# VectorE's late routing work between parts of its expert loop, and two weight parts and x0's low rows moved in the prologue

## The chip, the cores and the metric

The kernel runs on one core of one Trainium2 chip. The metric is the device time of one execution in microseconds; the kernel before takes 1338.12 us as the median of 3 runs (1337.47 to 1338.19).

## What is computed

The reference is one encoder layer over 512 tokens of width 1024, in float32, and a final norm:

```
h = x + W_out [ ConformerConv(xn) ; NeighbourhoodAttn2D(xn) ] + b_out,   xn = rmsnorm(x)
xt = rmsnorm(h);  logits = xt @ w_router + b_router
top 4 of 32 experts for each token, gates = softmax of the four logits
gt = min(xb @ w_gate[e] + b_gate[e], 7);  up = clip(xb @ w_up[e] + b_up[e], -7, 7)
y  = ((up + 1) * gt * sigmoid(1.702 gt)) @ w_down[e] + b_down[e]
h  = h + sum over the four experts of gate * y;   out = rmsnorm(h)
```

Each expert has three 1024 x 1024 float32 matrices, 12 MB; all 32 experts are read once, about 403 MB.

## The kernel before

**Stages.** Up to about 215 us the kernel does the input projections, the convolution and the attention. Then PE multiplies by W_out, tile by tile (`project_attn`, `project_conv`), VectorE adds the residual and norms (`residual`, `norm2`), PE turns the tiles and computes the router's logits, and VectorE picks the four best (`top`). From these VectorE sorts the experts by their token counts (big ones at even places of the order, small ones of at most 64 tokens at odd places), works out for each token and expert its rank, its block and its place in the block, and PE turns one-hot matrices into a token table (`table`). The expert part follows.

**Pieces.** An expert's weights are 12 pieces of 1 MB: 4 of gate, 4 of up, 4 of down. SyncE loads a piece into `w_raw` (`load`, line 486); ScalarE casts it to fp32r, `w_high` (`high_part`, line 833, a ring of 4 places, so it is at most 3 pieces ahead of PE); VectorE subtracts, `w_low` = `w_raw` - `w_high`, in place (`low_part`, line 1283). PE then takes three products for a piece of a big expert, high x high, low x high, high x low (`piece`, lines 1936 to 1938), and two for a piece of a small one (`piece_small`, lines 1952 and 1953). There are 12 buffers of raw pieces; SyncE reloads a buffer when PE counts its piece as used (`piece_used`).

**The order of the expert part.** Each engine has its instructions in an order written out by hand, and the engines meet at semaphores. Gate and up of expert 0 come first (a peeled stretch), then a pass for each expert j: gate and up of j+1, then down of j. Even and odd passes differ (`dve_even`, `dve_odd` on VectorE, `act_even`, `act_odd` on ScalarE), and a loop of 14 turns takes a pair each; the last passes are peeled again. GpSimd gathers the next expert's tokens with an indirect DMA, PE transposes them, ScalarE and VectorE split them into high and low rows (`xT_low_part`, for expert 0 `x0T_low`).

**What the change touches.** In the prologue: ScalarE's `high_part(1, 0, 1)` stands after the third tile's work and `high_part(2, 0, 2)` after the last tile's; VectorE's `low_part(1, 1)` stands between `xn2T_first(3)` and `top(2)`; `low_part(2, 2)` and `xT_low_part(0)` stand after the rank chain (`packed_i`, `parts_i`, `pos`), ahead of the one-hot matrices. ScalarE loads b_down over the bias staging area (line 842) before the first `square2`, and g_final (line 893) after the softmax of the gates. In the peeled stretch of expert 0 VectorE runs, beside its low parts: `dense_gates` (i = 0), `list_overflow` (i = 1, lines 1444 to 1451), `order_experts` (i = 2, lines 1565 to 1577), `split_down_bias` (i = 3, line 1455). In pass 0 it runs `late_onehots` (lines 1607 to 1610). Only the end of the kernel reads what these make (the addition of the experts' rows, the overflow blocks, the bias of down), but for `dense_gates`. SyncE waits for `list_overflow` before it loads piece 10 of expert 0.

Of the kernel before, what the change touches and what calls it, by code (L numbers as in the profile page):

```python
# [5 lines left out]
F32 = mybir.dt.float32  # L6
# [8 lines left out]
P = 128  # L15
SEQ, D_MODEL = 512, 1024
# [44 lines left out]
def encoder_kernel(nc, x, g_mix, w_in, b_in, conv_w, conv_b, ln_g, ln_b, rpb, w_out, b_out,  # L61
# [3 lines left out]
    with ctx:  # L65
# [90 lines left out]
        def split_parts(g):  # L156

            if g >= 16:
# [36 lines left out]
        gffn_row = area_v[:, 0:1024]  # L195
        gfin_row = area_a[:, 0:1024]
        xg = area_m[:, 0:1024]
        row_order = [(0, n) for n in range(NQ)] + [(r, n) for n in range(NQ) for r in range(1, TOP_K)]
# [31 lines left out]
                                   for i, name in enumerate(("first_slot", "pos_i", "slot")))  # L230
        ovf_exp = over("ovf_exp", t_at, 2048 + 3 * NJ, [1, MAX_OVERFLOW], I32)

        slot_of_rank = over("slot_of_rank", t_at, 2128, [P, NJ], I32)
# [3 lines left out]
        rank_j = area_t[:, 2128 + 4 * NJ + 64:2128 + 5 * NJ + 64]  # L237
        place_j, rank, first_j, extra_j, is_extra, blk, pos, tmp_j = (area_q[:, NJ * i:NJ * (i + 1)] for i in range(8))
        key, key_junk, place_off = (area_k[:, 32 * i:32 * i + 32] for i in range(3))
# [5 lines left out]
        parts_i = over("parts_i", k_at, 336, [P, 3, NJ], I32)  # L245
        counts, n_extra, first_extra, ovf_exp_f = (area_q[:, 128 + 32 * i:160 + 32 * i] for i in range(4))
        ovf_exp_f = ovf_exp_f[0:1, 0:MAX_OVERFLOW]
        cum = area_q[:, 256:256 + 4 * N_EXPERTS].rearrange("p (b e) -> p b e", b=2)

# [84 lines left out]
        wout_low_ready = sem("wout_low_ready")  # L334
        wout_done = sem("wout_done")
        wout_high_ready = sem("wout_high_ready")
        conv_high_ready = sem("conv_high_ready")
# [119 lines left out]
        def _(sp):  # L457
# [54 lines left out]
            for i in range(GATE, DOWN):  # L512
                if i == UP:
                    sp.wait_ge(overflow_ready, 2)
                    sp.wait_ge(gate_rows_ready, 1)
                    load(10, 0)
                reload(i, second, i)
# [174 lines left out]
        def _(act):  # L692
# [146 lines left out]
            s.copy(bias_gu[64:128, :], bias_stage[64:128, :]).then_inc(bias_high, 1)  # L839
            act.wait_ge(bias_split, 2)  # L840
            for i in range(4):
                act.dma_start(bias_stage[32 * i:32 * i + 32, :], b_down[0]).then_inc(bias_rows_loaded, 16)

            def square2(n):
# [9 lines left out]
            def xn2T_half(n):  # L854
                act.wait_ge(xn2_transposed, 2 * n + 2)
                s.copy(xn2T[n // 2][:, n % 2, 4:8, :],
                       bank[2 * (n % 2) + 1][:, :].rearrange("p (k t) -> p k t", k=4)).then_inc(xn2T_act, 1)

            square2(0)
            square2(1)  # L860
# [8 lines left out]
            act.wait_ge(wout_done, 2 * NQ)  # L869
            high_part(1, 0, 1)  # L870
            xn2_out(3)
# [11 lines left out]

            high_part(2, 0, 2)
            act.wait_ge(logits_done, NQ)
# [6 lines left out]
            act.wait_ge(xn2_stored, 16 * NQ)  # L892
            act.dma_start(gfin_row, row_bcast(g_final, D_MODEL)).then_inc(norm_rows_loaded, 16)
            act.wait_ge(bias_rows_loaded, 128)
            s.copy(bias_d[:, :], bias_stage).then_inc(bias_high, 1)

# [121 lines left out]
            with act.Fori(0, N_EXPERTS // 2 - 2) as jj:  # L1018
                act_odd(2 * jj + 1)
                act_even(2 * jj + 2, jj + 1)  # L1020
            act_odd(N_EXPERTS - 3, turn_small=False)
            act_even(N_EXPERTS - 2, N_EXPERTS // 2 - 1, last=True)
# [32 lines left out]
        def _(dve):  # L1055
# [225 lines left out]
            def low_part(i, at, raw=0):  # L1281
# [9 lines left out]
                            ALU.subtract).then_inc(bias_split, 1)  # L1291

            dve.wait_ge(norm_rows_loaded, 16)
            dve.wait_ge(router_loaded, 32)
# [18 lines left out]
            xn2T_first(3)  # L1313
            low_part(1, 1)
            top(2)
# [83 lines left out]
            then(v.tensor_reduce(packed_f, picked, AX.X, ALU.add))  # L1399
            then(v.tensor_copy(packed_i[:, :], packed_f))  # L1400
            v.tensor_scalar(parts_i[:, 1, :], packed_i[:, :], 1023, None, ALU.bitwise_and)
            v.tensor_scalar(parts_i[:, 2, :], packed_i[:, :], 15, None, ALU.logical_shift_right)
            then(v.tensor_scalar(upper_i[:, :], packed_i[:, :], 10, None, ALU.logical_shift_right))
            then(v.tensor_scalar(parts_i[:, 0, :], upper_i[:, :], N_EXPERTS - 1, None, ALU.bitwise_and))
            then(v.tensor_copy(area_q[:, 0:3 * NJ], parts_i[:, :, :].rearrange("p a b -> p (a b)")))

# [3 lines left out]
            then(v.scalar_tensor_tensor(pos[:, :], extra_j[:, :], -float(CAP), rank[:, :], ALU.mult, ALU.add))  # L1410
            low_part(2, 2)
            dve.wait_ge(xg_transposed, 1)
            xT_low_part(0, x0T_high, x0T_low)
            v.tensor_tensor(pos_1h[:, :, :], across(iota_f[:, 0:CAP], NJ), wide(pos[:, :], CAP), ALU.is_equal).then_inc(onehots_ready, 1)
# [27 lines left out]
            def list_overflow():  # L1442
                dve.wait_ge(gate_rows_ready, 1)
                v.tensor_scalar(first_slot[:, :], blk[:, :], float(CAP), None, ALU.mult)
                v.tensor_copy(pos_i[:, :], pos[:, :]).then_inc(slot_ready, 1)

                v.tensor_copy(n_ovf[:, :], cum[0:1, cur, 2 * N_EXPERTS - 1:]).then_inc(overflow_ready, 1)
                seen = cmp[0:1, :].rearrange("p (b e) -> p b e", e=N_EXPERTS)
                then(v.tensor_tensor(seen, wide(iota_f[0:1, 0:MAX_OVERFLOW], N_EXPERTS), across(cum[0:1, cur, N_EXPERTS:], MAX_OVERFLOW), ALU.is_ge))
                then(v.tensor_reduce(ovf_exp_f[:, :], seen, AX.X, ALU.add))  # L1450
                v.tensor_scalar(ovf_exp[:, :], ovf_exp_f[:, :], N_EXPERTS - 1.0, None, ALU.min).then_inc(overflow_ready, 1)

            def split_down_bias():
                dve.wait_ge(bias_high, 3)
                v.tensor_tensor(bias_d[32:64, :], bias_stage[32:64, :], bias_d[32:64, :].bitcast(F32),
                                ALU.subtract).then_inc(bias_split, 1)
# [101 lines left out]

            def order_experts():
# [4 lines left out]
                ranks = iota_f[:, 0:TOP_K].unsqueeze(1).unsqueeze(3).to_broadcast([P, NQ, TOP_K, TOP_K])  # L1564
                ranked(v.scalar_tensor_tensor(slot_f, blk[:, :], float(CAP), pos[:, :], ALU.mult, ALU.add))
# [4 lines left out]
                ranked(v.tensor_tensor(flat_gates, flat_gates, tmp_j[:, :], ALU.mult))  # L1570
                ranked(v.tensor_tensor(slot_f, slot_f, tmp_j[:, :], ALU.mult))
                ranked(v.tensor_tensor(earlier, inner(rank_j), ranks, ALU.is_equal))
                ranked(v.tensor_tensor(picked_rank, earlier, inner(slot_f), ALU.mult))
# [5 lines left out]
            for i in range(DOWN):  # L1579
# [3 lines left out]
                if i == 0:  # L1583
                    dense_gates()
                if i == 1:
                    list_overflow()
                if i == 2:
                    order_experts()
                if i == 3:
                    split_down_bias()  # L1590
                if i == 5:
                    xS_low_part(1)
                if i == 4:
                    dve.wait_ge(bias_split, 3)
                    dve.wait_ge(gate_rows_turned, 1)
                    v.tensor_copy(gate_cols[:, :, :], bank[4].rearrange("p (n t) -> p n t", n=NQ)).then_inc(gate_cols_ready, 1)
# [9 lines left out]
            def late_onehots():  # L1606
                know(v.tensor_reduce(row_gate, bank[5][:, COLS:COLS + 4].rearrange("p (b s) -> p b s", b=2), AX.X, ALU.add))
                know(v.tensor_copy(row_tok, tok_tab[:, LATE:N_EXPERTS]))
                for n in range(NQ):
                    know(v.tensor_scalar(row_tile[:, :, n], row_tok, -float(n * P), None, ALU.add))  # L1610
# [18 lines left out]
            dve_even(0, 0)  # L1629
            with dve.Fori(0, N_EXPERTS // 2 - 2) as jj:  # L1630
                dve_odd(2 * jj + 1)
                dve_even(2 * jj + 2, jj + 1)
            dve_odd(N_EXPERTS - 3, turn_small=False)
# [54 lines left out]
        def _(pe):  # L1688
# [96 lines left out]
            def project_attn(n):  # L1785
# [348 lines left out]
```

## Time and profile before

| | |
|---|---|
| median of 3 runs | 1338.12 us |
| the profiled execution | 1338.11 us, span 1336.3 us |
| PE busy | 1269.6 us (95%) |
| VectorE (DVE) busy | 1227.8 us (92%) |
| ScalarE (ACT) busy | 972.3 us (73%) |
| moved by DMA | 473.31 MB, mean 354 GB/s |

Busy times are shares of the whole span, over stages with different limits; a busy PE is not PE at its peak, since the ends of matmuls are modelled. DMA share is the mean busy share of the core's 16 DMA engines. A time in brackets behind an instruction is how long its engine sat idle before it, and what ended that. All times of rows are from the span's start.

### The profile page before, as it was taken

To read this page: it belongs to the slowest core of one execution; us is meant where nothing else is said; L and a number is where in the kernel's file an instruction comes from. 1 tells how busy PE (TensorE), PEld (TensorE's weight loads), DVE (VectorE), ACT (ScalarE), POOL (GpSimd) and SP (SyncE) were. 2 spreads that over 40 slices of the span, in tenths; PEclk is the share of its full clock that TensorE was granted. 3 is DMA by queue.
4 is the path that set the end of the run, shared out by engine and by line. 5 is a ranking of instruction groups with operands and counts; after the bars stand their busy time and mean duration, and the time that the engine had idled before them with its cause. 6 is when DMAs were issued, how large, how long until landed. Compare 5 with 4: busy or idle time off the path is not lost.

```text
span 1336.3 us, 17611 instructions
## 1 busy us (share of the span) xinstructions
PE 1269.6 (95%) x5771; PEld 1011.6 (76%) x5771; DVE 1227.8 (92%) x1010; ACT 972.3 (73%) x788; POOL 182.7 (14%) x181
## 2 busy tenths in 40 slices
PE   4999889789999999999999999999999999999996
PEld 4887668667878778787777777878777777777775
DVE  6799956699999999999999999999999999999997
ACT  4241664448797978788888888797979787878762
POOL 5001000112010101010110102020101010101252
PEclk9999889889999999999999999999999999999999
DMA  9945401499999999999999999999999999999984
GB/s 284 389 170 142 157 1 52 150 365 400 397 401 422 409 421 409 419 410 421 409 420 409 417 410 422 408 418 414 409 419 411 422 409 418 407 419 421 408 319 157
DMA packets 83974, 473.31 MB, mean 354 GB/s; under 512 B 10059, under 2 KB 10358, under 8 KB 34790
## 3 DMA queue, kind: packets, MB, share of 16 engines
q1 hardware_dynamic: 71726, 436.57, 81.1%
q0 software_dynamic: 7072, 19.39, 4.6%
q10 hardware_dynamic: 5144, 16.93, 3.4%
q8 instruction: 18, 0.29, 0.1%
q14 instruction: 14, 0.11, 0.0%
HBM read 447.72 MB, written 29.33 MB: 357 GB/s over the span
## 4 chain that ended last, share of the span: by engine, by line
PE 69%; DVE 15%; DMA 6%; ACT 5%; issue 3%; ACTq 1%; SPq 0%; POOL 0%; DVEq 0%
PE pair L1936 14%; PE pair L1937 13%; PE pair L1938 13%; PE pair L1952 6%; PE pair L1953 6%; DMA w_raw<-in_w_up 6%; DVE w_low L1283 5%; DVE area_m L1134 4%; ACT w_high L833 2%; PE pair L1923 2%; PE pair L1971 2%; PE pair L1950 1%; PE pair L1714 1%; PE pair L1715 1%; PE pair L1716 1%
## 5 line engine op out<-in xcount | busy, mean ns | idle before, releaser
L1283 DVE TENSOR_TENSOR w_low<-w_raw,w_high 128x2048 fp32r<-128x2048 f32 x380 | 838.2, 2245 | 41.3 <-ACT w_high L833 40.0
L833 ACT CAST w_high<-w_raw 128x2048 fp32r<-128x2048 f32 x380 | 703.0, 1878 | 170.5 <-PE pair L1938 117.5
L1936 PE MATMUL pair<-w_high,xT_high 128*128 128x512 f32 x528 | 211.2, 400 | 0.0
L1937 PE MATMUL pair<-w_low,xT_high 128*128 128x512 f32 x528 | 206.6, 391 | 0.0
L1938 PE MATMUL pair<-w_high,xT_low 128*128 128x512 f32 x528 | 206.0, 390 | 0.0
L1952 PE MATMUL pair<-w_high,xS 128*128 128x512 f32 x450 | 183.3, 407 | 0.1
L1953 PE MATMUL pair<-w_low,xS 128*128 128x512 f32 x450 | 175.7, 390 | 0.0
L1936 PEld LDWEIGHTS pair<-w_high,xT_high 128*128 128x128 f32 x528 | 99.1, 188 | 31.9 <-issue 11.4
L1938 PEld LDWEIGHTS pair<-w_high,xT_low 128*128 128x128 f32 x528 | 99.2, 188 | 21.6
L1937 PEld LDWEIGHTS pair<-w_low,xT_high 128*128 128x128 f32 x528 | 99.2, 188 | 19.2
L1936 PE MATMUL pair<-w_high,hT_high 128*128 128x512 f32 x256 | 102.1, 399 | 11.1 <-DVE w_low L1283 11.1
L1952 PEld LDWEIGHTS pair<-w_high,xS 128*128 128x128 f32 x450 | 84.5, 188 | 21.8 <-issue 3.6
L1937 PE MATMUL pair<-w_low,hT_high 128*128 128x512 f32 x256 | 100.5, 393 | 0.0
L1938 PE MATMUL pair<-w_high,hT_low 128*128 128x512 f32 x256 | 100.3, 392 | 0.0
L1953 PEld LDWEIGHTS pair<-w_low,xS 128*128 128x128 f32 x450 | 84.6, 188 | 20.4 <-issue 3.6
L1952 PE MATMUL pair<-w_high,hS 128*128 128x512 f32 x240 | 95.0, 396 | 0.0
L1953 PE MATMUL pair<-w_low,hS 128*128 128x512 f32 x240 | 93.5, 389 | 0.0
L1134 DVE SCALAR_TENSOR_TENSOR area_m<-area_u,convT,area_m 128x512 f32<-128x512 f32 x120 | 84.0, 755 | 0.4
L615 POOL CAST sel_in<-is_expert 128x128 fp32r (+1 forms) x17 | 42.6, 2504 | 272.0 <-PE pair L1953 246.9
L1936 PEld LDWEIGHTS pair<-w_high,hT_high 128*128 128x128 f32 x256 | 48.4, 189 | 23.7 <-DVE w_low L1283 12.2
L618 POOL CAST shift_sel<-is_expert 64x64 fp32r x15 | 14.1, 938 | 362.3 <-PE pair L1938 354.1
L1938 PEld LDWEIGHTS pair<-w_high,hT_low 128*128 128x128 f32 x256 | 48.5, 189 | 10.4
(355 smaller groups left out, 1800.5 us busy)
## 6 DMA issues: line engine op xcount, KB each, us to landing
w_raw<-in_w_gate SPq DMA_DIRECT2D x128, 1024.0 KB, 15.5
w_raw<-in_w_up SPq DMA_DIRECT2D x128, 1024.0 KB, 16.9
w_raw<-in_w_down SPq DMA_DIRECT2D x128, 1024.0 KB, 16.8
ring<-in_w_in SPq DMA_DIRECT2D x5, 2048.0 KB, 18.7
y_rows<-area_t SPq DMA_DIRECT2D x1, 8704.0 KB
y_rows<-area_m ACTq DMA_DIRECT2D x15, 512.0 KB
ring<-in_w_out SPq DMA_DIRECT2D x2, 2048.0 KB, 7.9
y_rows<-area_t SPq DMA_DIRECT2D x1, 3840.0 KB, 38.6
```

The lines of the kernel that those rows point to most:

```text
L615: g.tensor_copy(sel_in[:, :], is_expert[:, bass.ds(e, 1)].to_broadcast([P, CAP])).then_inc(sel_in_ready, 1)
L618: g.tensor_copy(shift_sel[SMALL:, SMALL:], is_expert[SMALL:, bass.ds(e, 1)].to_broadcast([SMALL, SMALL])).then_inc(sel_in_ready, 1)
L833: s.copy(w_high[:, i % HIGH_RING, raw:], w_raw[i][:, raw:]).then_inc(high_ready, 1)
L1134: v.scalar_tensor_tensor(mixedT[:, c, :], u_pad[:, c, k:k + SEQ], convT[:, k * CC + c:k * CC + c + 1], mixedT[:, c, :], ALU.mult, ALU.add) ...
L1283: v.tensor_tensor(w_low[i][:, raw:], w_raw[i][:, raw:], w_high[:, i % HIGH_RING, raw:].bitcast(F32), ALU.subtract).then_inc(low_ready, 1)
L1923: last = t.transpose(bank[6 + k // 4][:, (k % 4) * CAP:(k % 4 + 1) * CAP], h_tok[:, k::KD], ident[0:CAP, 0:CAP])
L1936: t.matmul(to[half], tok_high, hi, start=(opens and kk == 0), stop=False)
L1937: t.matmul(to[half], tok_high, lo, start=False, stop=False)
L1938: last = t.matmul(to[half], tok_low, hi, start=False, stop=(k == KD - 1))
L1952: t.matmul(to[half], rows, w_high[:, i % HIGH_RING, cols], start=(opens and kk == 0), stop=False)
L1953: last = t.matmul(to[half], rows, w_low[i][:, cols], start=False, stop=(k == KD - 1))
L1971: t.matmul(to[half], sel[:, :], rows[:, half * HALF:(half + 1) * HALF], start=True, stop=False)
```

## The change

Five things are done:

- VectorE's loop of 14 pairs is cut into six loops (3, 2, 3, 2, 2 and 2 pairs). Between them stand `late_rows` (the last five instructions of the old `late_onehots`), `list_overflow`, `order_by_rank` and `slots_by_rank` (together the old `order_experts`), and `split_down_bias`. What they read and write moves from area_q to area_v and area_t, where the loop doesn't overwrite it.
- The cast and the subtraction of weight piece 1 move ahead of the first `square2` and the first residual, behind a new semaphore that PE raises when the attention half of W_out is done. Those of piece 2 take the place that piece 1's had.
- `xT_low_part(0)` moves up, ahead of the unpacking of the ranks.
- SyncE no longer waits for the overflow list before it loads piece 10.
- The load of b_down moves into the place of that of g_final, into a part of area_a (`down_stage`); that of g_final goes behind ScalarE's loop. PE waits for the bias split only before it opens the output tiles.

```
@@ SyncE
                 if i == UP:
-                    sp.wait_ge(overflow_ready, 2)
                     sp.wait_ge(gate_rows_ready, 1)
                     load(10, 0)
@@ ScalarE, before the first square2
-            act.wait_ge(bias_split, 2)
-            for i in range(4):
-                act.dma_start(bias_stage[32 * i:32 * i + 32, :], b_down[0]).then_inc(bias_rows_loaded, 16)
+            act.wait_ge(attn_projected, NQ)
+            high_part(1, 0, 1)
             square2(0)
...
             act.wait_ge(wout_done, 2 * NQ)
-            high_part(1, 0, 1)
+            high_part(2, 0, 2)
             xn2_out(3)
             xn2T_half(3)
-            high_part(2, 0, 2)
...
             act.wait_ge(xn2_stored, 16 * NQ)
-            act.dma_start(gfin_row, row_bcast(g_final, D_MODEL)).then_inc(norm_rows_loaded, 16)
+            act.wait_ge(xn2_transposed, 2 * NQ)
+            for i in range(4):
+                act.dma_start(down_stage[32 * i:32 * i + 32, :], b_down[0]).then_inc(bias_rows_loaded, 16)
             act.wait_ge(bias_rows_loaded, 128)
-            s.copy(bias_d[:, :], bias_stage).then_inc(bias_high, 1)
+            s.copy(bias_d[:, :], down_stage).then_inc(bias_high, 1)
@@ ScalarE, behind its loop
+            act.wait_ge(bias_split, 3)
+            act.dma_start(gfin_row, row_bcast(g_final, D_MODEL)).then_inc(norm_rows_loaded, 16)
             act_odd(N_EXPERTS - 3, turn_small=False)
@@ VectorE
+            low_part(1, 1)
             dve.wait_ge(norm_rows_loaded, 16)
...
             xn2T_first(3)
-            low_part(1, 1)
+            low_part(2, 2)
             top(2)
...
             then(v.tensor_copy(packed_i[:, :], packed_f))
+            dve.wait_ge(xg_transposed, 1)
+            xT_low_part(0, x0T_high, x0T_low)
             v.tensor_scalar(parts_i[:, 1, :], packed_i[:, :], 1023, None, ALU.bitwise_and)
...
-            low_part(2, 2)
-            dve.wait_ge(xg_transposed, 1)
-            xT_low_part(0, x0T_high, x0T_low)
             v.tensor_tensor(pos_1h[:, :, :], ...).then_inc(onehots_ready, 1)
...
                 if i == 0:
                     dense_gates()
-                if i == 1:
-                    list_overflow()
-                if i == 2:
-                    order_experts()
-                if i == 3:
-                    split_down_bias()
...
             dve_even(0, 0)
-            with dve.Fori(0, N_EXPERTS // 2 - 2) as jj:
-                dve_odd(2 * jj + 1)
-                dve_even(2 * jj + 2, jj + 1)
+            def dve_pairs(first, end):
+                with dve.Fori(first, end) as jj:
+                    dve_odd(2 * jj + 1)
+                    dve_even(2 * jj + 2, jj + 1)
+
+            dve_pairs(0, 3)
+            late_rows()
+            dve_pairs(3, 5)
+            list_overflow()
+            dve_pairs(5, 8)
+            order_by_rank()
+            dve_pairs(8, 10)
+            slots_by_rank()
+            dve_pairs(10, 12)
+            split_down_bias()
+            dve_pairs(12, N_EXPERTS // 2 - 2)
@@ PE, project_attn
-                        t.matmul(to, attn_low[:, k, tokens], wout_high[half][:, 4 + k, :], start=False, stop=False)
+                        last = t.matmul(to, attn_low[:, k, tokens], wout_high[half][:, 4 + k, :], start=False, stop=False)
+                last.then_inc(attn_projected, 1)
@@ PE, before the output tiles
             pe.wait_ge(late_1h_ready, 1)
+            pe.wait_ge(bias_split, 3)
```

## Rows read from the trace of the kernel before

**Rows 1.** The page: DMA busy tenths in 40 slices; DMA issues.

```profile
DMA  9945401499999999999999999999999999999984
...
area_a<-in_g_final ACTq DMA_DIRECT2D x1, 512.0 KB, 3.8
area_m<-xn_rows,tok_now POOLq DMA_INDIRECT x32, 8.8
```

**Rows 2.** Windows: length, busy times, PE clock, DMA share, GB/s.

```profile
288.00:290.00 2.00, 2.00 (x11) 1.63 (x10) 1.93 (x4) 1.26 (x1) 1.01 (x1) 1.00 0.85 197
...
350.00:1270.00 920.00, 910.51 (x4088) 725.35 (x4087) 879.00 (x463) 774.62 (x506) 117.01 (x89) 1.00 1.01 414
```

**Rows 3.** DMA issues in 363:426, 900:963, 1128:1192; last number: us to landing.

```profile
w_raw<-in_w_gate SPq DMA_DIRECT2D x8, 1024.0 KB, 9.6
...
w_raw<-in_w_gate SPq DMA_DIRECT2D x8, 1024.0 KB, 19.3
...
w_raw<-in_w_gate SPq DMA_DIRECT2D x8, 1024.0 KB, 21.2
```

**Rows 4.** The chain that ended last: start us, us, what.

```profile
384.22 1.93 ACT w_high L833
...
447.49 1.92 ACT w_high L833
...
1081.27 1.92 ACT w_high L833
...
1145.69 1.92 ACT w_high L833
...
1186.19 19.20 DMA w_raw<-in_w_up
```

**Rows 5.** Waits in 1128:1192: total us, times, longest.

```profile
ACT w_high L833 <- DMA w_raw<-in_w_gate: 1.8, 3, 1.0
```

**Rows 6.** Timeline 268 to 275: start, us, engine, line, op, tiles.

```profile
268.98 1.01 ACT L951 CAST x0T_high<-pair 128x1024 fp32r<-128x1024 f32 x1 [8.15 <-PE pair L1916]
269.03 0.18 DVE L1400 CAST packed_i<-area_k 128x16 int32<-128x16 f32 x1
...
270.73 2.29 DVE L1283 TENSOR_TENSOR w_low<-w_raw,w_high 128x2048 fp32r<-128x2048 f32 x1
272.94 1.22 DVE L1342 TENSOR_TENSOR x0T_low<-pair,x0T_high 128x1024 fp32r<-128x1024 f32 x1
...
274.21 0.80 PE L1936 MATMUL pair<-w_high,x0T_high 128*128 128x512 f32 x1 [4.12 <-DVE x0T_low L1342]
```

**Rows 7.** Timeline: instructions that waited, in six places.

```profile
240.87 0.69 DVE L1197 TENSOR_TENSOR h<-h,pair 128x512 f32<-128x512 f32 x1 [1.08 <-PE pair L1807]
...
297.29 1.16 PE L1916 MATMUL pair<-ident,area_m 128*128 128x128 f32 x8 [0.54 <-DMA area_m<-xn_rows,tok_now]
...
309.51 1.16 PE L1923 MATMUL pair<-ident,area_q 128*128 128x128 f32 x8 [1.09 <-DVE area_q L1485]
...
325.25 0.47 PE L1936 MATMUL pair<-w_high,hT_high 128*128 128x512 f32 x1 [1.63 <-DVE w_low L1283]
...
355.23 2.29 DVE L1283 TENSOR_TENSOR w_low<-w_raw,w_high 128x2048 fp32r<-128x2048 f32 x1 [1.29 <-ACT w_high L833]
...
1227.13 1.92 ACT L833 CAST w_high<-w_raw 128x2048 fp32r<-128x2048 f32 x1 [0.51 <-DMA w_raw<-in_w_gate]
```

**Rows 8.** Timeline of VectorE: the routing work inside expert 0.

```profile
287.57 0.17 DVE L1444 TENSOR_SCALAR first_slot<-area_q 128x16 int32<-128x16 f32 x1
...
289.23 2.27 DVE L1283 TENSOR_TENSOR w_low<-w_raw,w_high 128x2048 fp32r<-128x2048 f32 x1
...
294.35 2.28 DVE L1283 TENSOR_TENSOR w_low<-w_raw,w_high 128x2048 fp32r<-128x2048 f32 x1
...
296.66 1.22 DVE L1455 TENSOR_TENSOR bias_d<-area_m,bias_d 32x1024 fp32r<-32x1024 f32 x1
...
322.00 0.79 DVE L1610 TENSOR_SCALAR small<-small 128x2 f32<-128x2 f32 x4
```

More of the change, by code:

```diff
@@ L196, in encoder_kernel @@
         gfin_row = area_a[:, 0:1024]
+        down_stage = area_a[:, 0:1024]
         xg = area_m[:, 0:1024]
@@ L231, in encoder_kernel @@
         ovf_exp = over("ovf_exp", t_at, 2048 + 3 * NJ, [1, MAX_OVERFLOW], I32)
+        seen = area_t[0:1, 2320:2320 + MAX_OVERFLOW * N_EXPERTS].rearrange("p (b e) -> p b e", e=N_EXPERTS)
         slot_of_rank = over("slot_of_rank", t_at, 2128, [P, NJ], I32)
@@ L237, in encoder_kernel @@
         rank_j = area_t[:, 2128 + 4 * NJ + 64:2128 + 5 * NJ + 64]
-        place_j, rank, first_j, extra_j, is_extra, blk, pos, tmp_j = (area_q[:, NJ * i:NJ * (i + 1)] for i in range(8))
+        place_j, rank, first_j, extra_j, is_extra, blk, pos, tmp_j = (area_v[:, NJ * i:NJ * (i + 1)] for i in range(8))
         key, key_junk, place_off = (area_k[:, 32 * i:32 * i + 32] for i in range(3))
@@ L245, in encoder_kernel @@
         parts_i = over("parts_i", k_at, 336, [P, 3, NJ], I32)
-        counts, n_extra, first_extra, ovf_exp_f = (area_q[:, 128 + 32 * i:160 + 32 * i] for i in range(4))
-        ovf_exp_f = ovf_exp_f[0:1, 0:MAX_OVERFLOW]
-        cum = area_q[:, 256:256 + 4 * N_EXPERTS].rearrange("p (b e) -> p b e", b=2)
+        counts, n_extra, first_extra = (area_q[:, 128 + 32 * i:160 + 32 * i] for i in range(3))
+        ovf_exp_f = area_v[0:1, 768:768 + MAX_OVERFLOW]
+        cum = area_v[:, 640:640 + 4 * N_EXPERTS].rearrange("p (b e) -> p b e", b=2)
         ident = sb("ident", [P, P])
@@ L335, in encoder_kernel @@
         wout_done = sem("wout_done")
+        attn_projected = sem("attn_projected")
         wout_high_ready = sem("wout_high_ready")
@@ L1404, in _ @@
             then(v.tensor_scalar(parts_i[:, 0, :], upper_i[:, :], N_EXPERTS - 1, None, ALU.bitwise_and))
-            then(v.tensor_copy(area_q[:, 0:3 * NJ], parts_i[:, :, :].rearrange("p a b -> p (a b)")))
+            then(v.tensor_copy(area_v[:, 0:3 * NJ], parts_i[:, :, :].rearrange("p a b -> p (a b)")))
             past = cmp[:, 0:NJ * EXTRA].rearrange("p (i t) -> p i t", i=NJ)
@@ L1447, in list_overflow @@
                 v.tensor_copy(n_ovf[:, :], cum[0:1, cur, 2 * N_EXPERTS - 1:]).then_inc(overflow_ready, 1)
-                seen = cmp[0:1, :].rearrange("p (b e) -> p b e", e=N_EXPERTS)
                 then(v.tensor_tensor(seen, wide(iota_f[0:1, 0:MAX_OVERFLOW], N_EXPERTS), across(cum[0:1, cur, N_EXPERTS:], MAX_OVERFLOW), ALU.is_ge))
@@ L1454, in split_down_bias @@
                 dve.wait_ge(bias_high, 3)
-                v.tensor_tensor(bias_d[32:64, :], bias_stage[32:64, :], bias_d[32:64, :].bitcast(F32),
+                v.tensor_tensor(bias_d[32:64, :], down_stage[32:64, :], bias_d[32:64, :].bitcast(F32),
                                 ALU.subtract).then_inc(bias_split, 1)
@@ L1557, in ranked, with order_by_rank @@
                 dve.wait_ge(rank_step, n_ranked[0])
-            def order_experts():
+            def order_by_rank():
                 by_tile = lambda ap: ap.rearrange("p (n j) -> p n j", n=NQ)
@@ L1563, in order_experts @@
                 outer = lambda ap: by_tile(ap).unsqueeze(3).to_broadcast([P, NQ, TOP_K, TOP_K])
-                ranks = iota_f[:, 0:TOP_K].unsqueeze(1).unsqueeze(3).to_broadcast([P, NQ, TOP_K, TOP_K])
                 ranked(v.scalar_tensor_tensor(slot_f, blk[:, :], float(CAP), pos[:, :], ALU.mult, ALU.add))
@@ L1571, in order_experts, with slots_by_rank @@
                 ranked(v.tensor_tensor(slot_f, slot_f, tmp_j[:, :], ALU.mult))
+            def slots_by_rank():
+                by_tile = lambda ap: ap.rearrange("p (n j) -> p n j", n=NQ)
+                inner = lambda ap: by_tile(ap).unsqueeze(2).to_broadcast([P, NQ, TOP_K, TOP_K])
+                ranks = iota_f[:, 0:TOP_K].unsqueeze(1).unsqueeze(3).to_broadcast([P, NQ, TOP_K, TOP_K])
                 ranked(v.tensor_tensor(earlier, inner(rank_j), ranks, ALU.is_equal))
@@ L1593, in _ @@
                 if i == 4:
-                    dve.wait_ge(bias_split, 3)
                     dve.wait_ge(gate_rows_turned, 1)
@@ L1607, in late_onehots, with late_rows @@
                 know(v.tensor_reduce(row_gate, bank[5][:, COLS:COLS + 4].rearrange("p (b s) -> p b s", b=2), AX.X, ALU.add))
+            def late_rows():
                 know(v.tensor_copy(row_tok, tok_tab[:, LATE:N_EXPERTS]))
```

## The prediction

> **What bounds the kernel now.** I read the page first, then one long window, then landing times, then the chain of waits. The reader is to see in the page's slices that the 16 DMA engines are as busy as they can be from the eighth slice nearly to the end [rows 1], and in one window over 350 to 1270 us a share of 1.01 and 414 GB/s, without pause, while PE is busy for 910.5 of 920 us [rows 2]. Two things look like the bound. The landing times tell them apart: a 1 MB gate piece lands 9.6 us after its issue at 363 to 426 us, 19.3 us at 900 to 963, 21.2 us at 1128 to 1192 [rows 3]. The transfers fall behind steadily, (19.3 - 9.6) / (537 / 63.3) = 1.14 us for each pair of experts. The chain gives the same from the other side: the cast and the subtraction that end a PE stretch recur at 384.22 and 447.49, 63.27 us apart; late in the loop at 1081.27 and 1145.69, 64.42 us apart, 1.15 more, and a load of 19.2 us stands in the chain itself [rows 4]. Late in the loop ScalarE waits for gate pieces [rows 5]; the same view has no such wait at 900 to 963 us and has it from 1000 to 1064 on. So PE sets the pace of the loop to about 1000 us and lives on a store of early loads; when the store is spent, the DMA stream sets it. The end depends on when that stream starts, how much it carries, and where it stands idle. What makes PE earlier only spends the store sooner.
>
> The stream starts with the six loads that SyncE issues once the first gather has landed. The one hole afterwards is 288 to 290 us, share 0.85 and 197 GB/s [rows 2]: the first loads are through, and the next wait for PE to free buffers.
>
> **The change, part by part.** Durations are from the profiled execution: span 1336.3, its own time 1338.11, so 1.8 us around the span; the median of the runs is 1338.12, and no correction is needed.
>
> *Weight part 1 to before the residuals.* It costs VectorE 2.2 us ahead of the first residual (2.29 us a piece, as at 270.73 in [rows 6]). The first two residuals and the first norm move by about 1 us. PE is busy with the conv projection then, and the residual at 240.87 waited 1.08 us for PE [rows 7], so the delay is gone before it; ends 0 and +1.0, taken 0. ScalarE's cast for it falls into a wait. Part 2 takes part 1's place between the top-four searches, same size, so the routing and the first gather are where they were.
>
> *Weight part 2 out of the rank chain, x0's low rows ahead of it.* The subtraction of part 2 at 270.73 (2.29 us) goes; x0's low rows waited behind it till 272.94, and PE's first product till 274.21 [rows 6]. Its input, ScalarE's cast of 268.98 (1.01), is there at 270.0. VectorE is free after packed_i at 269.03 + 0.18 = 269.2, so it now stalls 0.8 us, does the low rows to 271.2, and PE starts at 271.25: 2.96 us earlier. The rank chain behind it gains 2.2 - 0.8 = 1.4 us, and so do the token table and the second gather.
>
> *Routing work out of the first expert.* From 287.57 to 289.23 the overflow list (1.66 us); from 289.23 + 2.20 to 294.35 the thirteen rank operations (2.9); at 296.66 the bias split (1.22); the four of 322.00 and the cast before them (0.79 + 0.2) [rows 8]: 6.8 us less on an engine that the chain follows there. PE's transposes at 297.29 waited for the second gather, which moves by only 1.4 us; behind it two waits of PE for VectorE go, 1.09 and 1.63 us [rows 7]. PE is then 1.4 + 2.7 = 4.1 us ahead at 325 us, if the loads of the second expert's up pieces, late next, are there; I take 4. None of it is in the sum, for the reason above.
>
> *What it gives the stream.* PE uses its first piece 3 us earlier, so SyncE's reloads come 3 us earlier and the hole at 288 is filled. By share it is (1.01 - 0.85) x 2 = 0.3 us, by bytes (414 - 197) x 2 / 414 = 1.05 us [rows 2]. I take 0.6. SyncE's dropped wait for the overflow list gives nothing: it stands behind the reload of gate piece 3, which waits for PE longer.
>
> *The same work between the loops.* The blocks cost VectorE 1.0, 1.7, 1.5, 1.4 and 1.2 us, each at the end of a pair. Queued behind are the next low parts; the first wait after such a place is 1.29 us at 355.23 [rows 7], and ScalarE's store of casts covers the rest. Cost 0; if the cover were short, at most 1.7 us once, and the PE lead pays for it.
>
> *DMAs.* b_down (512 KB) moves from 227 us to 259 us, where g_final's 512 KB stood: the same load before the first gather, 0 to +0.5, taken 0. g_final, 3.8 us to landing in a quiet stretch [rows 1], moves to ScalarE's exit from its loop, about 1226.6 us, into the full stream: 0.524 MB / 414 GB/s = +1.27 us for every load then under way. The last cast that waits for a load is the one at 1227.13 [rows 7]; after it the casts wait for PE, since the last experts' pieces take three products each. Ends 0 and +1.27; I take 0, nearest to that row.
> The Trainium skill (Trainium Kernel Development and Optimization, Key Constraints) says that transfers issued by different engines share the same 16 DMA engines, so that another queue saves nothing but issue time. By that rule alone g_final costs its full 1.27 us and the sum is 0.7 us slower, not 0.6 faster.
>
> **Sum:** -0.6 + 0 = -0.6 us: 1338.11 - 0.6 = 1337.5.
>
> **The rivals.**
> *A, the lead is carried to the end.* For it: the chain between 280 and 325 us is VectorE nearly throughout, and 4 to 5 us go from it. Against it: the landing times of [rows 3]. The lead of 4 us is 4 / 1.15 = 3.5 pairs, so the wait for loads should begin some 225 us sooner, near 775, and nothing be left. If the growth of landing times were only a result of PE's pace, the time would be 1338.1 - 4.5 = 1333.6.
> *B, g_final is not hidden.* For it: ScalarE waits for loads right up to 1227.13. Against: the waits for PE after it. Time 1338.11 - 0.6 + 1.27 = 1338.8.
> *C, slower: code loading in the new loops.* VectorE's one loop becomes six copies of its body, and instructions have to be fetched. If one copy does not stay loaded, VectorE stalls in each pass. The trace has no fetch of that kind; the nearest is a gather through the full stream, 8.8 us from issue to landing [rows 1]; less the 1.29 us wait that it would fill, 7.5 us a pass, 22.5 in three passes, and 0 if it is hidden. It decides from the point where PE's loss exceeds its cover: 4 us of new lead and 3 pairs x 1.15 = 3.5 us that PE waits for loads late in the loop, 7.5 in all. Time at the dear end 1338.1 + 22.5 - 7.5 = 1353, slower from 7.5 us of stalls on. Against: the present loop runs 14 passes without a wait of that kind, and a short stall costs nothing.
> The Trainium skill (Runtime: NRT & Kernel Launch, Instruction fetch mechanics) states that a taken branch to code outside the two pages held forces a fetch; by it, a stall each pass needs a body that is not within two pages. No row here shows such a stall.
>
> **How the numbers follow.** Forecast 0.66, own range 1337.0 to 1338.4 (the hole from 1.05 to 0.3, b_down up to 0.5). A 0.14, B 0.13, C 0.07. Forecast and B make 0.79; the range goes down to 1334.6 for a lead carried in part, and up to 1339.6 for B with b_down's delay. A measurement of this kernel tells about 0.2% (2.7 us) from no change. Faster by more is A and a little: 0.15. Slower by more is C: 0.07. Within: 0.78.
>
> **What would show it.** PE's first product of the first expert at 271.2 instead of 274.2. The hole at 288 to 290 us gone. PE some 4 us ahead at 325 us. Landing times of gate pieces higher by about 4 us at equal windows (near 14 at 363 to 426), the same top of about 21, and ScalarE's waits for loads beginning near 775 us; the period 64.4 us from there. If those times don't rise and the last period stays 63.3, A is right and I am wrong. A wait of VectorE for no engine at a loop's start would be C; casts waiting for loads after 1230 us would be B.

## The result and the profile after

The changed kernel takes 1339.41 us (median of 18 runs, 1337.76 to 1341.27) beside 1337.3 for the kernel before in the same session: ratio 1.0017, 95% interval 1.0011 to 1.0024, so 2.3 us slower. The forecast was 0.6 us faster, 1337.5 for 1338.11. In all ratios below, a thousandth is 1.34 us; three executions of 1436, 1597 and 3367 us, far over all others, are left out of them. The profiled execution is at the upper end of its runs (1341.27 us, span 1339.5), so times of day in it are compared with those of before only within about 1 us.

The page after, and windows of the same stretches as [rows 1, 2]:

```profile
DMA  9945401499999999999999999999999999999983
...
q14 instruction: 17, 0.14, 0.0%
```

```profile
288.00:290.00 2.00, 2.00 (x10) 1.64 (x10) 2.00 (x2) 1.98 (x2) 1.42 (x1) 1.00 1.03 334
350.00:1000.00 650.00, 645.90 (x2902) 515.01 (x2901) 626.91 (x354) 548.22 (x360) 81.38 (x63) 1.00 1.01 413
1000.00:1200.00 200.00, 194.68 (x868) 153.88 (x867) 189.70 (x101) 166.76 (x109) 23.76 (x18) 1.00 1.01 412
```

The hole at 288 to 290 us is gone, and the queue of code loads (q14) has 17 packets where the kernel before has 14. The start of the first expert, as in [rows 6] (timeline: start, us, engine, line, operation, tiles, idle before it and what ended that):

```profile
270.23 1.23 DVE L1346 TENSOR_TENSOR x0T_low<-pair,x0T_high 128x1024 fp32r<-128x1024 f32 x1 [0.81 <-ACT x0T_high L952]
...
271.51 0.80 PE L1950 MATMUL pair<-w_high,x0T_high 128*128 128x512 f32 x1 [1.31 <-DVE x0T_low L1346]
...
287.11 2.32 POOL L606 DMA_INDIRECT area_m<-xn_rows,tok_now  x1 [2.66 <-issue]
...
297.35 1.97 PE L1930 MATMUL pair<-ident,area_m 128*128 128x128 f32 x8 [3.60 <-DMA area_m<-xn_rows,tok_now]
...
354.31 2.29 DVE L1286 TENSOR_TENSOR w_low<-w_raw,w_high 128x2048 fp32r<-128x2048 f32 x1 [1.24 <-ACT w_high L835]
```

PE has its first product 2.7 us earlier, and the second gather is issued 1.2 us earlier (287.11 for 288.32). But PE's transposes behind that gather start at 297.35, where they started before at 297.29 [rows 7]. Of the 4 us of lead that were forecast for 325 us, 0.9 are there at 354 us (354.31 for 355.23, [rows 7]).

The end is where the loss is seen. ScalarE in 1225 to 1242 us, and its waits from 1200 to 1290 (total us, times, longest), first before, then after:

```profile
1225.94 0.36 ACTq L1023 DMA_DIRECT2D area_a<-in_g_final  x1
...
1231.81 1.91 ACT L835 CAST w_high<-w_raw 128x2048 fp32r<-128x2048 f32 x1 [0.80 <-DMA w_raw<-in_w_up]
1235.37 1.92 ACT L835 CAST w_high<-w_raw 128x2048 fp32r<-128x2048 f32 x1 [1.65 <-DMA w_raw<-in_w_up]
...
1238.92 1.90 ACT L835 CAST w_high<-w_raw 128x2048 fp32r<-128x2048 f32 x1 [1.15 <-DMA w_raw<-in_w_up]
```

```profile
ACT w_high L833 <- PE pair L1938: 11.3, 13, 1.7
ACT w_high L833 <- DMA w_raw<-in_w_gate: 1.0, 2, 0.5
ACT w_high L833 <- DMA w_raw<-in_w_up: 0.9, 2, 0.6
```

```profile
ACT w_high L835 <- DMA w_raw<-in_w_up: 7.3, 9, 1.7
ACT w_high L835 <- DMA w_raw<-in_w_gate: 3.5, 4, 1.4
ACT w_high L835 <- DMA w_raw<-in_w_down: 3.5, 5, 1.2
ACT w_high L835 <- PE pair L1952: 1.2, 2, 0.8
...
ACT w_high L877 <- DMA w_raw<-in_w_down: 0.5, 1, 0.5
```

Before, 1.9 us of waits for loads in that window; after, 14.8. The casts had waited for PE up to the end; now they wait for the stream. The chain says the same: it has a load of the last experts in it, which it had not.

```profile
1058.68 19.15 DMA w_raw<-in_w_up
...
1123.13 19.11 DMA w_raw<-in_w_up
...
1187.51 18.90 DMA w_raw<-in_w_up
...
1256.34 24.89 DMA w_raw<-in_w_down
```

The load at 1187.51 stands at 1186.19 in [rows 4]: the loss has two parts, one before 1058 us and one behind 1226.

### The profile page after: what moved, and what is told of

Its sections match the earlier page's. It is cut to its first block, busy times and chain, and to the rows that moved or that the text cites. A ratio compares the mean times of both kernels' runs of the same rounds, so it can differ in the third digit from the quotient of the medians.

```text
span 1339.5 us, 17616 instructions
## 1 busy us (share of the span) xinstructions
PE 1272.4 (95%) x5771; PEld 1013.4 (76%) x5771; DVE 1228.0 (92%) x1010; ACT 972.5 (73%) x788; POOL 175.2 (13%) x181
## 4 chain that ended last, share of the span: by engine, by line
PE 69%; DVE 11%; DMA 9%; ACT 5%; issue 4%; ACTq 1%; SPq 0%; POOLq 0%; POOL 0%; DVEq 0%
PE pair L1950 14%; PE pair L1951 13%; PE pair L1952 13%; PE pair L1966 6%; PE pair L1967 6%; DMA w_raw<-in_w_up 6%; DVE w_low L1286 4%; DVE area_m L1137 4%; ACT w_high L835 2%; PE pair L1937 2%; DMA w_raw<-in_w_down 2%; PE pair L1985 1%; PE pair L1964 1%; PE pair L1727 1%; PE pair L1728 1%
```

## The experiments

Each kernel has 11 or 12 runs beside 15 to 35 of the kernel before in the same session; experiment 3 has 5, the two of experiment 12 one each. The brackets are 95% intervals, so a difference of two ratios is uncertain by some 1.5 us. "Copies" are those of VectorE's loop, "blocks" the routing work between them, "moves" the weight parts ahead of the sort and x0's low rows ahead of the ranks.

**1. g_final's load alone.** The kernel before, with:

```
-            act.dma_start(gfin_row, row_bcast(g_final, D_MODEL))...   # behind the gates, 259 us
+            act.dma_start(gfin_row, row_bcast(g_final, D_MODEL))...   # behind ACT's loop, 1226 us
```

> The kernel before, with one line moved: the load of g_final goes behind ScalarE's loop. Theory S (the load in the full DMA stream costs the time, everything else of the change is neutral): slower than before by 1.3 us (its bytes) to 2.3 us (the shift of landing times seen in the changed kernel's tail), and ScalarE's casts wait for loads after 1230 us. Rival V (VectorE's blocks between the loops and the six copies of the body cost it): no change, within 0.5 us. Rival P (the moves in the prologue cost it): no change.

Ratio 1.0008 (0.9999 to 1.0017), +1.1 us with an interval that reaches 0. Behind 1200 us its casts wait 10.0 us for loads:

```profile
ACT w_high L833 <- DMA w_raw<-in_w_up: 4.6, 7, 1.0
ACT w_high L833 <- DMA w_raw<-in_w_gate: 2.7, 3, 1.7
ACT w_high L833 <- DMA w_raw<-in_w_down: 2.1, 2, 1.5
...
ACT w_high L877 <- DMA w_raw<-in_w_down: 0.6, 1, 0.6
```

**2. The changed kernel without that.** The same load behind the last high part, `high_last(3, TAIL + 3)`, where the stream has run empty:

> The changed kernel with g_final loaded only after ScalarE's last weight cast but one, when the loads are through. Theory S: the loss goes, the time is 1.5 to 2.5 us below the changed kernel's, so at or up to 1 us below the kernel before. Rival V and rival P: it stays 2 us slower than before.

1.0005 (0.9996 to 1.0014), with 6.7 us of waits for loads behind 1200. So g_final's place is one part, 1.0017 - 1.0005 = 1.6 us, and probably not the whole: the time is no longer told from that of the kernel before, but the waits still stand over 1.9.

**3. The moves alone**, b_down's four loads left at 227 us:

```
+            act.wait_ge(attn_projected, NQ)
+            high_part(1, 0, 1)          # ACT, behind b_down's issues, ahead of square2(0)
+            low_part(1, 1)              # DVE, ahead of the residuals
```

> The kernel before with only the moves in the prologue (weight parts 1 and 2, x0's low rows, the semaphore behind the attention half). Theory S with the DMA stream as the bound: within 1 us of before, though PE's first product of expert 0 is 3 us earlier. Rival P: slower by 1 to 2 us. If PE's lead counted: faster by 1 us or more.

1.0041 (1.0028 to 1.0055), 5.5 us slower. Its timeline:

```profile
228.19 1.73 ACTq L843 DMA_DIRECT2D area_m<-in_b_down  x4
230.02 1.91 ACT L834 CAST w_high<-w_raw 128x2048 fp32r<-128x2048 f32 x1 [4.37 <-issue]
...
231.96 2.29 DVE L1285 TENSOR_TENSOR w_low<-w_raw,w_high 128x2048 fp32r<-128x2048 f32 x1 [3.81 <-ACT w_high L834]
```

The cast now stands behind ScalarE's wait for the bias split and four issues, and the low part and all residuals behind it are late: the first residual pair begins at 234.17, in the changed kernel at 229.65. The move is free only because b_down leaves the queue ahead of it. The run also shows how a delay travels. The loads of the second loop pass are issued 4.9 us late (358.22, before 353.27), and late in the loop the loads in the chain are as late, 1062.11 and 1191.00 for 1057.41 and 1186.19:

```profile
1062.11 19.14 DMA w_raw<-in_w_up
1126.52 19.21 DMA w_raw<-in_w_up
1191.00 18.92 DMA w_raw<-in_w_up
```

**4. The blocks with their copies**, b_down's move, g_final at the tail, without the moves:

> The changed kernel without the moves in the prologue, g_final loaded at the tail: only the routing work between the loops (and b_down's place) is left. Theory S: within 1 us of before. Rival V: slower by 1 to 2 us, and VectorE waits for no engine where a new loop begins.

1.0001 (0.9991 to 1.0010). VectorE has 6.8 us less in expert 0 and the kernel is no faster. In its trace PE starts its first product of expert 1 (hT_high) 3.4 us before the kernel before (321.88 for 325.25), of which 1.4 us were there at its first product of all (272.77 for 274.21); the last reloads, behind 1260 us, are issued 1.4 us earlier. So the 2.0 us that the shorter VectorE work gave PE are gone by the end.

**5. The changed kernel without blocks and copies:**

```
+                if i == 1: list_overflow()
+                if i == 2: order_by_rank(); slots_by_rank()
+                if i == 3: split_down_bias()
-            dve_pairs(0, 3) ... dve_pairs(12, N_EXPERTS // 2 - 2)
+            dve_pairs(0, N_EXPERTS // 2 - 2)
```

> The changed kernel with g_final loaded behind the last high part, and the routing work back in expert 0 and one loop again; left are the moves ahead of the sort and of the ranks, and b_down behind the stores. Nothing is left out. Theory S (the load stream carries the end, each part adds its own piece: blocks and copies +1.0 at the end, g_final +2.0): the end gets back 1.0 against the kernel with the blocks, 1336.5 to 1337, a ratio of 0.9994 to 0.9998. Theory B (the low parts' move costs by itself, because the reloads start 3 us earlier and delay the second gather): 1337.5 to 1338.5, over 1.0003. If the earlier start of the stream is carried whole: 1335.5.

0.9987 (0.9978 to 0.9996): faster than before, and 2.4 us faster than experiment 2, where a gain of 1.0 over it had been expected. Run again with experiments 10 and 11:

> The changed kernel without the blocks once more, beside the two that take it apart. Nothing is left out. If it beats the kernel before, the ratio is again 0.998 to 0.9995; if the first result was chance, 0.9997 to 1.0005.

0.9995 (0.9986 to 1.0004). The gain over experiment 2 stands (mean of the two 0.9991, 1.9 us), the one over the kernel before is not sure. The same step without the moves, from experiment 11 (0.9997, below) to experiment 4 (1.0001), is only 0.5 us: blocks and copies together cost 0.5 to 1.9 us, about 1.2.

**6. Two more loads of g_final** in the kernel before, at expert 0 and ahead of ScalarE's loop:

> The kernel before with g_final loaded two more times into the same row buffer, once in the stretch of expert 0 and once ahead of ACT's loop: 1 MB more in the stream of 384 pieces of 1 MB (2 x 0.5 MB, spread over the partitions), nothing else changed and nothing left out. Theory S (the stream is the bound from some 1000 us on and every byte ahead of that is carried to the end): one piece lasts 2.66 us in the steady stretch, so +2.0 to +2.7 us, a ratio of 1.0015 to 1.0020. Theory L (the stream has slack until the last experts, so that what is added early is absorbed): +0 to +0.3 us, 0.9998 to 1.0002.

1.0016 (1.0007 to 1.0026), +2.1 us: theory S. Gate pieces land 0.9 us later at 363 to 426 us and 1.0 later at 900 to 963, and no later at 1128 to 1192 (10.5, 20.3, 21.1 for the 9.6, 19.3, 21.2 of [rows 3]): the store of early loads is smaller by what was added, and then it is used up sooner.

```profile
w_raw<-in_w_gate SPq DMA_DIRECT2D x8, 1024.0 KB, 10.5
...
w_raw<-in_w_gate SPq DMA_DIRECT2D x8, 1024.0 KB, 20.3
...
w_raw<-in_w_gate SPq DMA_DIRECT2D x8, 1024.0 KB, 21.1
```

**7. Copies with nothing between them**, in the kernel before:

```
+            for first, end in ((0, 3), (3, 5), (5, 8), (8, 10), (10, 12), (12, N_EXPERTS // 2 - 2)):
-            with dve.Fori(0, N_EXPERTS // 2 - 2) as jj:
+                with dve.Fori(first, end) as jj:
```

> The kernel before with VectorE's loop of 14 turns cut into six loops of 3, 2, 3, 2, 2 and 2 turns, with nothing between them: only the copies of the code. Nothing is left out. Theory C (the loading of code for six loop bodies costs, through the queue of code loads or a stall at each entry): pieces 60 to 348 take 0.7 to 1.3 us longer and the end comes 0.5 to 1.3 later, a ratio of 1.0004 to 1.0010. Theory W (the work between the loops, not the copies, costs what the kernel with the blocks lost): no difference, 0.9998 to 1.0002, and the queue of code loads has more packets all the same.

1.0011 (1.0002 to 1.0021), +1.5 us for code alone. It too has 17 packets in q14. The trace puts the three more at 662, 975 and 1168 us. In the windows around the first (down pieces, last number us to landing; 575 to 640, then q14 in 655 to 670, then 670 to 733):

```profile
w_raw<-in_w_down SPq DMA_DIRECT2D x8, 1024.0 KB, 13.9
...
q14 instruction: 1, 0.01, 0.1%
...
w_raw<-in_w_down SPq DMA_DIRECT2D x8, 1024.0 KB, 16.6
```

The kernel before has no packet there and goes from 13.9 to 15.6:

```profile
w_raw<-in_w_down SPq DMA_DIRECT2D x8, 1024.0 KB, 13.9
...
w_raw<-in_w_down SPq DMA_DIRECT2D x8, 1024.0 KB, 15.6
```

A step of 1.0 us in the landing, right behind an 8 KB packet that itself took 0.31 us. Piece by piece, from the trace's landing records, the last of the 16 landings of a piece (one for each DMA engine) steps up, against the kernel before, by 0.9, 0.8 and 0.9 us at the three packets; elsewhere between 450 and 1000 us it moves by 0.5 us at most and comes back. At 662 us the other fifteen landings stay within 0.2 us: one packet, one engine. In the kernels with blocks (2 and 4) the steps stand at their packets, at 678 to 684, 978 to 981 and 1230 to 1234 us; the last of these goes with their longer waits for loads behind 1200 (6.7 and 6.6 us). Experiment 7 has no added packet there and waits 1.6 us; experiment 9 has one at 1234 us and waits 5.5.

**8. Three pieces earlier:** pieces 5, 6, 7 right behind 3 and 4 on SyncE's queue, not behind the gather:

> The kernel before with pieces 5, 6 and 7 issued right behind 3 and 4 on SyncE's queue (at some 247 us) and not behind the two gathers (from 267 us on); 8, 9 and 11 stay where they are. Nothing is left out. Theory S (the stream carries the end): three pieces of 2.66 us each are out of the way while the queues were idle, so up to 8 us less to move later; as the reloads can only start when a buffer is read, the gain is bounded by the hole ahead of piece 12: 1.5 to 3 us faster, 1334.5 to 1336, a ratio of 0.998 to 0.999. Theory L: PE is bound by the first gathers and products, and the lead is lost by 1000 us: no difference. A price on the other side: the gather at 262 us queues behind 3 MB on all 16 DMA engines and lands up to 8 us late; then PE starts late and the whole is 3 to 6 us slower.

1.0003 (0.9993 to 1.0012), no difference. In the trace up piece 5 is issued 18.3 us earlier, but the first gate reloads, some 283 us, 0.5 us later than before. With experiment 3 this says what the end hangs on: not when the first loads are issued, but when PE reaches the even pace of the loop; from there each reload follows PE's reading.

**9. Fourteen copies:**

> The kernel before with VectorE's loop of 14 turns written out as 14 copies of one turn each, nothing between them: only code. Nothing is left out. Six copies gave three more packets of 8 KB in the queue of code loads (17 for 14), each with a step of some 0.85 us in the latency of the slowest DMA engine, and +1.5 us. Theory C (each code packet ahead of the end takes its time from the slowest DMA engine, and the stream carries it): 13 more copies at 3/5 packet each are 7 to 8 more packets, +4 to +6.5 us, 1341 to 1343.5, a ratio of 1.003 to 1.005. Theory E (the entry into a cold copy stalls VectorE, once per copy, whatever the queue carries): 13/5 of 1.5 us as well if it is carried, but then the waits of TensorE for VectorE grow at the entries and the latency of the loads shows no steps. Theory N (the +1.5 of six copies was chance): within 0.1% of before.

1.0015 (1.0005 to 1.0025), +2.0 us. The size was missed: not 7 or 8 more packets but 4 (18 in q14), at 558, 785, 1002 and 1234 us. By copies it does not fit (13 more copies against 5 would have been 3.9, above the interval); by packets it can, 3 for 1.5 us and 4 for 2.0, but with about 1.3 us of uncertainty on each, and its last landings were already 1.9 us above those of the kernels without added packets at 530 us, ahead of the first of the four. The packet at 558 left no step, that at 785 one of 0.5, the other two 0.9 each. Theory E is out: from 400 to 800 us, over seven entries into a new copy, PE waits for low parts 2.4 us, as in the kernel before, and from 350 to 1230 us every idle stretch of VectorE of over 0.25 us is ended by another engine's work, here and in experiment 7.

**10. g_final at the tail alone**, the one line moved in the kernel before:

> The kernel before with only g_final's load moved, from 259 us to behind the last high part, where the queues run empty. Nothing is left out. Theory G (the 0.5 MB at 259 us costs, because they stand ahead of the gather and the first reloads and are carried): 0.5 to 1.3 us faster, a ratio of 0.9990 to 0.9996, and what the changed kernel without the blocks gained is mostly this. Theory P (its gain is that of the parts moved ahead of the sort and the ranks): no difference, 0.9998 to 1.0002.

**11. Experiment 5 without the moves**, which are taken back as in experiment 3's diff:

> The changed kernel without the blocks (g_final at the tail, routing work in expert 0) and without the moves ahead of the sort and of the ranks: left against the kernel before are b_down's later load, the removed wait of SyncE and g_final at the tail. Nothing is left out. Theory P (the moves gain): within 0.2 us of before or the gain of g_final alone, 1336 to 1337, and 1 us over the kernel with the moves. Theory G: as fast as the kernel with the moves, a ratio of 0.998 to 0.9995.

Experiments 10 and 11 came out at 0.9994 (0.9985 to 1.0003) and 0.9997 (0.9988 to 1.0006), with 0.9995 for experiment 5 beside them. All three are a little under 1 and none is told from it or from the others. The question between theories G and P stays open. The moves are 0.9991 - 0.9997 = -0.8 us here and, from experiment 4 to experiment 2, 1.0005 - 1.0001 = +0.5: nothing is shown for them either way. Against experiment 1, g_final at 1226 us costs 1.0008 - 0.9994 = 1.9 us over the tail, beside 1.6 from experiment 2. Behind 1200 us these kernels wait for loads 1.9 to 2.0 us, as before.

**12. One row and sixteen rows** loaded behind ScalarE's loop in the kernel before, one run each, so their times (1335.25 and 1335.39) say nothing and only the waits and landings are read:

> The kernel before with one packet more in the stream's last stretch: behind ACT's loop (some 1226 us) it loads one row of g_final, 4 KB, into the first partition of the row buffer, which holds the same numbers already. Nothing is left out. A code packet of 8 KB at 1230 us went with 1.0 us more latency of the slowest DMA engine and with 6.7 us of ACT's waits for w_raw in the window 1200 to 1290, where the kernel before has 1.9. Theory K (what costs is any small packet on the engine that is late, several times its own 0.16 to 0.33 us): 3 to 6 us of those waits. Theory B (bytes alone): 0.16 us more latency, the waits stay at 1.7 to 2.3. The place of the partition decides which DMA engine takes it: if it isn't the late one, theory B's picture comes also under K.

> The same with 16 rows, 64 KB. Nothing is left out. If the 16 rows go to 16 engines, one packet each, K expects 3 to 6 us of ACT's waits for w_raw in 1200 to 1290 and B 1.9 to 2.5; if they all go to one engine, both expect over 3 us. The whole load of 128 rows gave 10.0 us of these waits and 1.3 us of latency (1 us of the time).

One row: waits of 1.8 us, no step. Sixteen rows: 3.7 us, and the last landing of a piece steps by some 0.75 us (landing records). 128 rows, eight times the bytes, were 10.0 us and a step of 1.6 that grows to 2.3. First one row, then sixteen:

```profile
ACT w_high L833 <- DMA w_raw<-in_w_gate: 0.9, 2, 0.7
ACT w_high L833 <- DMA w_raw<-in_w_up: 0.9, 2, 0.6
```

```profile
ACT w_high L833 <- DMA w_raw<-in_w_up: 2.0, 4, 0.8
ACT w_high L833 <- DMA w_raw<-in_w_gate: 1.7, 3, 0.7
```

So the price doesn't go by bytes alone: 64 KB are 0.16 us at 414 GB/s. The records of the sixteen-row load show 16 packets of 4 KB, of 0.16 to 0.44 us, and 16 landings of its own, from 1226.91 to 1228.18, so the rows went one to each engine. Of the 16 landings of a weight piece, the eight late ones (see the last section) step by 0.7 to 1.1 us with it, but for one, and the eight early ones by 0.16 at most: a 4 KB packet costs a late engine over its own time. Which engine took the single row isn't shown; it may have met one with time to spare.

**13. All blocks in one place**, between two loops of seven passes, g_final at the tail:

```
+            dve_pairs(0, 7)
+            late_rows(); list_overflow(); order_by_rank(); slots_by_rank(); split_down_bias()
+            dve_pairs(7, N_EXPERTS // 2 - 2)
```

> The changed kernel with g_final at the tail and all routing blocks in one place, between two loops of seven turns: two copies of the loop for six. Nothing is left out. Theory C (code packets): 15 or 16 packets in the queue of code loads for 17, one step of 0.8 us in the loads' latency at the most, and a time between the kernel without the blocks (1336.3) and the one with six copies (1337.8): 1336.5 to 1337.3, a ratio of 0.9996 to 1.0001. Theory W (VectorE's work between the loops costs): all the work in one stop of some 20 instructions makes it as slow or slower, 1337.8 or more, over 1.0004, and TensorE waits for VectorE at the cut (some 700 us).

1.0026 (1.0017 to 1.0035), the slowest arrangement of the blocks, with 15 packets only: theory W, for a lump. From 783.16 to 790.12 VectorE does nothing for the loop, 7.0 us, and PE waits:

```profile
783.16 0.17 DVE L1608 CAST small<-tok_tab 128x2 f32<-128x2 int32 x1
...
788.87 1.22 DVE L1457 TENSOR_TENSOR bias_d<-area_a,bias_d 32x1024 fp32r<-32x1024 f32 x1
790.12 6.70 DVE L1286 TENSOR_TENSOR w_low<-w_raw,w_high 128x2048 fp32r<-128x2048 f32 x3
...
792.46 0.79 PE L1946 MATMUL pair<-w_high,xT_high 128*128 128x512 f32 x1 [5.05 <-DVE w_low L1286]
```

5.05 of 7.0 us go through, so the cover there is about 2 us, and blocks of 1.0 to 1.7 fit under it. In 400 to 985 us PE waits for low parts 3.6 us in the kernel before and 3.6 in experiment 2, first row and second; in this one 8.7:

```profile
PE pair L1936 <- DVE w_low L1283: 3.6, 9, 0.4
```

```profile
PE pair L1950 <- DVE w_low L1286: 3.6, 9, 0.5
```

A PE stall of 5.0 us became 3.5 us of time against the kernel before. Against experiment 5, the same kernel with this work in expert 0, it is 1.0026 - 0.9991 = 4.7 us, nearly the whole. In its last stretch no cast waits for a load any more. So PE's own chain had ended only about 0.3 to 1.5 us ahead of the stream, which is within what the ratios can tell.

## Why the prediction was wrong

*What bounds the kernel: right in the main.* The stream sets the end, with PE close behind (experiment 13). Experiment 6 adds 1 MB early and pays 2.1 us; 1.05 MB / 414 GB/s is 2.5. In the changed kernel ScalarE's waits for loads begin sooner (0.4 us in 850 to 936, 3.5 in 936 to 1000, before none and 0.6), though not near 775 us as forecast. But "What makes PE earlier only spends the store sooner" was too strong: experiments 3 and 8 show a shift of PE's start carried whole and a shift of the first loads worth nothing.

*g_final in the full stream, taken 0, is 1.6 to 1.9 us over the tail: the first failed term.* The step said that the last cast that waits for a load is the one at 1227.13 and that after it the casts wait for PE. That was true of the row and wrong as a bound: those 13 waits for PE were 0.9 us each in the mean and 1.7 at most, and a load that makes every piece under way 1.6 us later, and some 2.3, turns them into waits for loads. Against the kernel before, where the same move also frees the place at 259 us, it is 1.1 us and not told from 0 (experiment 1); in the changed kernel b_down fills that place. Rival B had the mechanism, with 1.27 us; its 0.13 was too little. The rule of the Trainium skill (Trainium Kernel Development and Optimization, Key Constraints), that another engine's transfer saves nothing but the issue, was weighed there and set aside; the trace agrees with it. Whether the time is more than the 1.27 us of the bytes the runs don't tell, but the landings moved by more.

*The blocks, "Cost 0", are 0.5 to 1.9 us with their copies: the second failed term.* The step looked for the cost on VectorE and there it was right: no stall, as experiment 13 shows from the other side. The cost is code, as far as the ratios tell. Experiment 7 has it without any work, +1.5 us (0.3 to 2.8). Rival C looked at code and looked for a stall of VectorE in each pass, 7.5 us a pass; there is none. VectorE enters the copies of experiment 7 at 528, 655, 844, 971 and 1100 us; the added packets stand at 662, 975 and 1168 us and at no wait of VectorE. So the fetch is hidden from it, but not from the 16 DMA engines that the end waits for. The rows to see it in were the page's: q14's packets, and DMA at its full share.

*The gain, taken 0.6 by the hole, was not there as such.* PE's first product came 2.7 us earlier (predicted 2.96), the hole closed, and the gather was issued 1.2 us earlier (predicted 1.4). The step that failed is that PE's transposes would follow: the gate reloads are issued 2.7 us earlier (277.19 for 279.89), the hole is closed, and the gather lands when it did before. That it queues behind these reloads is the likely reason; no run isolates it. PE's lead was 0.9 us, not 4, and the gate pieces of 363 to 426 us landed after 10.1 us, not 14. Experiment 5 (mean of its two ratios) against 11 puts the moves at -0.8 us, which would be that lead, but experiment 2 against 4 puts them at +0.5.

*The sum.* Along one line of kernels (before, experiment 11, 5, 2, changed): b_down, SyncE's wait and g_final at the tail -0.4; the moves -0.8; blocks and copies 0.9991 to 1.0005, +1.9; g_final to 1226 us +1.6; together +2.3. That they add up to the measured time proves nothing, since each is the difference to the next kernel of the line; by way of experiment 4 the middle two are +0.5 and +0.5. Each has an uncertainty of about 1.5 us. The two large ones are borne out by an independent pair each (experiment 1 against 10, +1.9; experiment 7, +1.5) and by the waits and landings; the two small ones are not. The change of 2.3 us itself was told from none to within 0.9 us, finer than the 2.7 that the prediction took. (In its own range, -0.3 + 0.5 give 1338.3 at the top, not 1338.4.)

The best version that came of it is experiment 5: the moves, with the routing work left in expert 0 and g_final at the tail. It is clearly faster than the changed kernel (0.9987 and 0.9995 against 1.0017). Against the kernel before, the first session says faster, the second does not tell.

## What to carry to other kernels

When the DMA stream sets the end, what adds bytes to it before the end can be on the path, however small its queue: here a 0.5 MB row and a few packets of code cost as much as the change could bring. Waits for another engine next to a resource that is nearly late are no cover; ask by how much the resource misses being the bound, piece by piece. And writing a loop out in copies, to put little work between them, is not free of charge because no engine stalls.

## What the hardware showed that I had not expected

An 8 KB packet of code that lasts 0.31 to 0.33 us moved the landing on the slowest DMA engine by 0.8 to 0.9 us, at all three places of experiment 7; one packet of experiment 9 moved nothing, and one 0.5 us. The number of such packets followed neither copies nor bytes of code in a simple way: 6 copies gave 3, 14 copies gave 4. Why a packet costs three times its own duration was not settled.

The late landing is not that of one engine. In the kernel before, the 16 landings of a gate piece come 7.0 to 8.9 us after its issue at 372 us; at 942 us eight of them come after 6.8 to 10.1 us and the other eight after 17.8 to 19.3 (landing records). Half of the engines keep pace, and the store of early loads is used up on the other half; the median landing times of [rows 3] are those of the last engine and don't show it. Why the halves differ was not settled.
